# Two-layer encoder trunk: the norm's reciprocal on 128 columns by way of DRAM, a copy moved to ScalarE, one early head fewer

## The reference

```python
def rms_norm(x, g):
    return x * lax.rsqrt(jnp.mean(x * x, axis=-1, keepdims=True) + 1e-6) * g

def swiglu(h, w_gate, w_up, w_down):
    return (jax.nn.silu(h @ w_gate) * (h @ w_up)) @ w_down

# layer 0: multi-head latent attention (8 heads, rope, block-causal mask)
# layer 1: bcx = h @ w_in; y = (B * causal_conv3(C * X)) @ w_out
for i in range(2):
    h = h + mixer_i(rms_norm(h, mixer_norm_i))
    h = h + swiglu(rms_norm(h, ffn_norm[i]), w_gate[i], w_up[i], w_down[i])
return rms_norm(h, final_norm)
```

## Time and profile before

| | |
|---|---|
| median of 3 runs | 1054.24 us (1054.06 to 1055.86) |
| the profiled execution, its own time | 1052.55 us |
| its span, first to last instruction | 1050.6 us |
| TensorE busy | 1041.8 us (99%), 7018 matmuls |
| VectorE busy | 908.9 us (87%) |
| ScalarE busy | 556.6 us (53%) |
| granted TensorE clock, mean | 0.999 |
| DMA | 106.29 MB, 101 GB/s |

### The profile page before, as it was taken

How to read it: one execution, slowest core, us unless ns; L and a number is a source line. 1 busy time by engine, 2 the same in 40 slices (tenths; PEclk the granted TensorE clock), 3 DMA queues, 4 the chain that set the end, 5 groups by cost and what they waited for, 6 DMA issues and landing times. The chain is left out here.

```text
span 1050.6 us, 18481 instructions
## 1 busy us (share of the span) xinstructions
PE 1041.8 (99%) x7018; PEld 959.4 (91%) x7018; DVE 908.9 (87%) x1291; ACT 556.6 (53%) x801; POOL 46.6 (4%) x28
## 2 busy tenths in 40 slices
PE   9999999999999999999999999999999999999998
PEld 7888888899999999889888999888999999988897
DVE  6787775999999998997879988699999999899685
ACT  6678883745554555633344434355555545563432
POOL 0342230000000000000000000000000000000000
PEclk9999999999999999999999999999999999999999
DMA  8121212233233233223222332322332232223212
GB/s 339 53 71 50 75 46 80 81 121 110 92 117 120 87 113 110 75 107 121 85 107 90 111 122 80 112 90 81 120 120 93 106 120 102 88 101 120 81 71 80
DMA packets 16972, 106.29 MB, mean 101 GB/s; under 512 B 1888, under 2 KB 2272, under 8 KB 6432
## 3 DMA queue, kind: packets, MB, share of 16 engines
q1 hardware_dynamic: 16416, 104.60, 27.7%
q10 hardware_dynamic: 432, 0.83, 0.2%
q0 software_dynamic: 80, 0.26, 0.1%
HBM read 103.59 MB, written 2.10 MB: 101 GB/s over the span
## 5 line engine op out<-in xcount | busy, mean ns | idle before, releaser
L511 PE MATMUL bank<-x_hi,split 128*128 128x256 f32 (+1 forms) x704 | 203.6, 289 | 0.1
L513 PE MATMUL bank<-x_hi,split 128*128 128x256 f32 (+1 forms) x704 | 203.4, 289 | 0.0
L512 PE MATMUL bank<-x_lo,split 128*128 128x256 f32 (+1 forms) x704 | 203.3, 289 | 0.0
L511 PEld LDWEIGHTS bank<-x_hi,split 128*128 128x128 f32 x704 | 132.3, 188 | 3.4 <-DVE split L1521 0.6
L511 PE MATMUL bank<-x_hi,s_hi 128*128 128x256 f32 x480 | 134.3, 280 | 0.4 <-ACT work L1238 0.4
L513 PEld LDWEIGHTS bank<-x_hi,split 128*128 128x128 f32 x704 | 132.3, 188 | 2.5
L512 PEld LDWEIGHTS bank<-x_lo,split 128*128 128x128 f32 x704 | 132.3, 188 | 2.5
L513 PE MATMUL bank<-x_hi,s_lo 128*128 128x256 f32 x480 | 133.9, 279 | 0.0
L512 PE MATMUL bank<-x_lo,s_hi 128*128 128x256 f32 x480 | 133.8, 279 | 0.0
L1903 DVE TENSOR_TENSOR split<-raw,split 128x2048 fp32r<-128x2048 f32 x54 | 123.6, 2289 | 11.7 <-ACT split L1228 10.6
L1228 ACT ACTIVATE split<-raw 128x2048 fp32r<-128x2048 f32 x54 | 103.4, 1916 | 46.2 <-PE bank L513 25.9
(11 more groups left out here) (289 smaller groups left out, 2469.9 us busy)
## 6 DMA issues: line engine op xcount, KB each, us to landing
raw<-weights_in SPq DMA_DIRECT2D x82, 1024.0 KB, 4.8
raw<-weights_in SPq DMA_DIRECT2D x12, 768.0 KB, 4.2
work<-x SPq DMA_DIRECT2D x4, 512.0 KB, 12.9
raw<-weights_in SPq DMA_DIRECT2D x4, 512.0 KB, 3.7
out<-head SPq DMA_DIRECT2D x3, 512.0 KB, 2.7
head<-head_in SPq DMA_DIRECT2D x1, 768.0 KB, 9.3
first_raw<-weights_in SPq DMA_DIRECT2D x3, 192.0 KB, 5.4
first_raw<-weights_in SPq DMA_DIRECT2D x1, 576.0 KB, 8.0
```

The lines of the kernel that those rows point to most:

```text
L511: pe.matmul(o, lhs[0], rhs[0], start=start, stop=False, skip_group_check=True)
L512: pe.matmul(o, lhs[0], rhs[1], start=False, stop=False, skip_group_check=True)
L513: return pe.matmul(o, lhs[1], rhs[0], start=False, stop=stop, skip_group_check=True)
```

## The change

- `rms` on ScalarE takes the square root of only a quarter of the equal rows for each quarter of the tokens: rows 0 to 31 of tokens 0 to 127, rows 32 to 63 of tokens 128 to 255, and so on, in four instructions of 32x128, into `rms_part` (128x128 in SBUF). The fourth also frees the bank. The convolution uses the same function.
- `inverse_rms` on VectorE takes the reciprocal of `rms_part`, 128x128.
- SP stores `rms_part` to `rms_rows` in DRAM (64 KB), waits for it, and loads one row of each quarter back on all 128 partitions into `rstd` (256 KB in pieces of 512 B). This is `spread_inverse`, on the queue that also loads the weights, behind the fourth weight chunk of the stage. VectorE waits for it in `inverse_spread`.
- VectorE does `forms_split(0)` between the reciprocal and the wait, in all three places.
- In the channel mixer's first round, ScalarE runs a Silu of 128x1 early, and its first `gate` is written out: copy of product 1, `blocks_hi(1)`, copy of product 5, sums, copy of product 6.
- At the start of the convolution ScalarE makes the two copies of banks 0 and 1 into `mix_b`, between the copies of products 5 and 6.
- TensorE multiplies three early heads, not four, between `heads` and the wait for banks 3 and 7; the fourth comes behind `chunk_done[0]`.

```diff
+            def spread_inverse():
+                n = T.add("inverse")
+                sp.wait_ge(rms_inverted, n)
+                sp.dma_start(rms_rows, rms_part[:, :]).then_inc(inverse_stored, 16)
+                sp.wait_ge(inverse_stored, 16 * n)
+                rows = rms_rows.rearrange("(q r) n -> q r n", q=TOK)[:, 0, :]
+                sp.dma_start(rstd[:, :].rearrange("p (q n) -> p q n", q=TOK), rows.partition_broadcast(P)).then_inc(rstd_landed, 16)
...
-                c = loads(c, KF // 2, [SLOT] * 2)
+                c = loads(c, 2, [SLOT] * 2)
+                spread_inverse()
+                c = loads(c, KF // 2 - 2, [SLOT] * 2)
...
-                    c = loads(c, 8, [SLOT] * 2)
+                    c = loads(c, 2, [SLOT] * 2)
+                    spread_inverse()
+                    c = loads(c, 6, [SLOT] * 2)
...
-            output(1, 1, early[:half + 1])
+            output(1, 1, early[:half])
...
-            output(1, 1, early[half + 1:])
+            output(1, 1, early[half:])
...
-                act.activation(bank[b][:, :], bank[b][:, :], ACT.Sqrt, bias=eps[:, 0:1], scale=1.0 / width).then_inc(rms_done, 1)
+                for q in range(TOK):
+                    rows, cols = slice(q * P // TOK, (q + 1) * P // TOK), slice(q * P, (q + 1) * P)
+                    part = act.activation(rms_part[rows, :], bank[b][rows, cols], ACT.Sqrt, bias=eps[rows, 0:1], scale=1.0 / width)
+                part.then_inc(drained[b], 1)
...
+                act.activation(silu_scratch[:, :], eps[:, :], ACT.Silu)
...
-                gate(copy_first=True)
+                copy(0, 1)
+                blocks_hi(1)
+                copy(0, 5)
+                sums_hi_of(1)
+                copy(0, 6)
+                copy_last(0, 0)
...
-            act.activation(rstd[:, :], bank[6][:, :], ACT.Sqrt, bias=eps[:, 0:1], scale=1.0 / D).then_inc(drained[6], 1)
+            rms(6, D)
...
             copy(0, 5)
+            act.wait_ge(chunk_done[1], T.now("slot1") - 1)
+            for b in range(2):
+                act.activation(mix_b[b], bank[b][:, :], ACT.Copy).then_inc(drained[b], 1)
             copy(0, 6)
...
             def inverse_rms(b):
-                v.wait_ge(rms_done, T.add("rms"))
-                drain(b, v.reciprocal(rstd[:, :], bank[b][:, :]))
-                landed(b)
+                v.wait_ge(drained[b], T.add(f"b{b}"))
+                v.reciprocal(rms_part[:, :], rms_part[:, :]).then_inc(rms_inverted, 1)
+
+            def inverse_spread():
+                v.wait_ge(rstd_landed, 16 * T.add("inverse"))
...
                 inverse_rms(4)
+                forms_split(0)
+                inverse_spread()
                 scaled(3, 0)
                 scaled(4, 1)
-                forms_split(0)
                 forms(1)
...
+            inverse_rms(6)
             forms_split(0)
-            v.wait_ge(drained[6], T.add("b6"))
-            do(v.reciprocal(rstd[:, :], rstd[:, :]))
-            settle()
+            inverse_spread()
             do(v.tensor_tensor(rstd2, rstd[:, :], rstd[:, :], ALU.mult))
             settle()
             drained_part(mix_y, 2, rstd2)
-            done(1)
             for b in range(2):
-                drain(b, v.tensor_copy(mix_b[b], bank[b][:, :]))
-            landed(0, 1)
+                T.add(f"b{b}")
             split(1)
             next_forms(0)
+            landed(0, 1)
```

More of the change, by code:

```diff
@@ L222, in build @@
         rstd = sb("rstd", SEQ)
+        rms_part = sb("rms_part", P)
+        rms_rows = nc.dram_tensor("rms_rows", (P, P), F32).ap()
         acc = sb("acc", SEQ)
@@ L231, in build @@
         eps, act_scratch = numbers[:, 9 * TOK:9 * TOK + 1], numbers[:, 9 * TOK + 1:9 * TOK + 2]
+        silu_scratch = numbers[:, 9 * TOK + 2:9 * TOK + 3]
         bank = [ctx.enter_context(nc.psum_tensor(f"bank{b}", [P, SEQ], F32)) for b in range(8)]
@@ L325, in build @@
         rms_done = sem("rms_done")
+        rms_inverted, inverse_stored, rstd_landed = sem("rms_inverted"), sem("inverse_stored"), sem("rstd_landed")
         silu_done = sem("silu_done")
@@ L1400, in _ @@
             T.add("x", K_PAIRS)
-            act.wait_ge(stat_summed, T.add("stat"))
-            act.activation(rstd[:, :], bank[6][:, :], ACT.Sqrt, bias=eps[:, 0:1], scale=1.0 / D).then_inc(drained[6], 1)
+            rms(6, D)
             banks_used(dict(b6=1))
```

## The result

The changed kernel takes **1064.62 us** (median of 5 runs, 1064.13 to 1066.57), the kernel before 1054.10 (5 runs). The ratio is 1.0106, with a 95% interval of 1.0094 to 1.0117: slower by 10.5 us, where 2.4 us faster was forecast. The profiled execution took 1064.62 us with a span of 1062.8, which is 12.1 and 12.2 us above the profiled one of before. The executions of one kernel fall into groups about 1.6 us apart (the kernel before: near 1052.5, 1054.1 and 1055.8 us), so where less than 2 us is at stake the spans of profiled executions out of the lowest group are given beside the medians.

A forecast was written before the change was run, and what follows sets the result against it. TensorE, busy 99%, was taken as the bound, so only its gaps counted: heads -0.3, channel mixers -0.45 and -0.9, convolution -0.7, say -2.4 us, from 1054.24 to 1051.8 us. Range 1050.8 to 1054.4 us.

The forecast's parts named there:

- What bounds, and where the gaps are: TensorE bounds; its reachable gaps cost 0.6 (heads), 0.45 and 0.9 (channel mixers, layers 0 and 1) and 0.7 us (convolution).
- Heads (-0.3): Heads' projection: the old gap of 0.6 us goes, a new wait costs 0.3, net -0.3 us.
- copies and convolution (-0.7): Convolution: ScalarE's two copies and the smaller reciprocal make VectorE earlier, so TensorE's gap near 593 us goes, -0.7 us.
- the 3.7 us: Convolution: VectorE's time saved, 3.34 and 1.29 us less 0.9 that comes back; half was allowed to be lost.
- Reciprocal: VectorE, channel mixers: with a quarter of the columns it takes 0.9 us, where it took 3.35.
- cover of 5.1 us: Channel mixers: VectorE's work from the reciprocal's end to the end of `forms_split` hides 5.1 us of the round trip.
- ScalarE's high part: Channel mixers: `forms_split` waits for it until 216.94 us, losing 1.1 of the 2.45 us saved on VectorE.
- SP's queue: The transfers stand between the stage's fourth and fifth weight chunks; the weight load isn't late, so they cost nothing.
- Store: Round trip: storing 64 KB takes 1.7 us, upper bound 2.75.
- The load: Round trip: loading 256 KB takes 3.15 us, bounds 2.6 and 6.8; with 0.4 and the store the trip is 5.3.
- The upper bound of 6.8: Round trip: the longest load time allowed, 6.8 us, from the only load that sends one row to all partitions.
- Rival 2: Channel mixers: beyond a trip of 6.4 us each further us comes back in both; at 10 us, 1061 us; chance 8%.

## Why the prediction was wrong

- **What bounds, and where the gaps are**: right. The gaps at 178 and 593 us went with one edit each, and the kernel with a quick trip lost those at 246 and 750 us as well.
- **Heads (-0.3), copies and convolution (-0.7)**: right in the traces; each is below what the time alone can tell. In the convolution the 1.3 us of the copies were enough, so the 3.7 us that were summed up there counted for no more.
- **Reciprocal, cover of 5.1 us, ScalarE's high part**: right, each within 0.1 us. The four square roots took 1.48 us, and only the convolution felt it (0.3 us).
- **SP's queue**: "the weight load isn't late". It was issued in time (219.5 us), but behind the slow row load it landed at 229.7, where before it was 226.7. No engine waited for it, so the term stays nothing.
- **Store**: "2.7 - 1.0 = 1.7", measured 1.5. The row decided rightly against the 2.15 that the prediction worked out by the Trainium skill, page "DMA: Bandwidth & Descriptors", section "Anatomy of one DMA". That formula is a fit on DMAs that GpSimd issues, and this store goes out from SP, so the 1.5 us do not contradict the page.
- **The load**: "3.7 - 0.55 = 3.15, by the nearest rows in queue and size". This is the step that failed. The load took 8.9 to 9.8 us in the change, so the round trip was 10.4 to 11.4 us and not 5.3. The term is right within 0.3 us where the four rows lie side by side, 1, 2 or 16.5 KB apart (3.3 to 3.4 us), and wrong at 4 KB (7.0), 8 KB (9.2) and the change's 16 KB (9.1 in the median). Why DRAM answers so stays open. The term treated the load as bytes and looked at queue and size; none of the rows that it was taken from reads one small piece of DRAM for all partitions with 8 or 16 KB between its rows. The upper bound of 6.8 came from the only row that did read a shared row, and even that is too low.
- **The range** left this case out by giving it 8%. Rival 2 had the mechanism and its place, and at its trip of 10 us it said 1061; the trip was 11.4 us in layer 0, 10.7 in the convolution and 10.4 in layer 1. Its price of one microsecond per microsecond in each channel mixer is about what layer 0 shows (4.6 us for 5.0 beyond 6.4); layer 1 shows 3.1 us of gaps for 4.0. It lacked the clock, which stretched layer 1 further, and it took 0.3 us for the convolution, whose gaps grew from 0.7 to 2.7 us.
- The Trainium skill's page "DMA: Bandwidth & Descriptors", section "Latency and other measured facts", has a row on large distances: copies whose rows lie 512 KiB apart run at 207 GB/s, at 2 MiB at 164, at 4 and 8 MiB at 103, and 4 KiB of padding to the 4 MiB brings back 214. I had read it as one on large distances only. These runs agree in kind, at distances of 4 to 16 KB; here 512 B more between the rows that are read (16 B of padding to each row) are enough.

## What to carry to other kernels

A term for an operation that the trace does not show needs its access pattern matched, not only its queue and its bytes; where no row does, the chance of the bad end is not small. Rows that all partitions read belong side by side in DRAM, or 16.5 KB apart rather than 16, for example; of the distances tried, exactly 4, 8 and 16 KB were the slow ones. And a change that fails may still be right in every other part: this one is faster than the kernel before by 0.35% with one row of 2 KB (1049.61 us, span 1047.9 against 1050.6) and by 0.48% with 16 B of padding to a row (1049.78 us).

## What the runs showed of the hardware that I had not expected

- A 256 KB load of four shared 512 B rows takes 3.3 us or 9.2 by the distance of the rows: 1, 2 and 16.5 KB quick, 8 and 16 KB slow, 4 KB 7.0 us.
- What stands behind such a load on the queue is held up with it: the next 1 MB of weights took 10.2 us to land in layer 0, where it took 4.7 in the kernel before, and 8.0 with rows 4 KB apart.
- A gap of 3.0 us on TensorE in layer 1 was followed by a lower granted clock (0.61 and 0.71, above); one as long in layer 0 of the same execution was not, and in the run with four rows 16 KB apart the clock fell in layer 0 as well. The windows view around the gap of layer 0, first of the change, then of that run:

```profile
225.00:235.00 10.00, 5.49 (x45) 5.10 (x44) 6.81 (x9) 5.22 (x7) 0.00 (x0) 1.00 0.24 99
```

```profile
226.00:236.00 10.00, 6.89 (x46) 6.40 (x45) 8.50 (x10) 5.36 (x7) 0.00 (x0) 0.83 0.14 58
```

- The fall of the clock costs less than the slow stretch itself, as part of it fills time in which TensorE would have waited for its next copy. In layer 0 the run with the lower clock had a second gap of 0.8 us in place of 1.9, and VectorE's second `forms_split` behind the load (L1934) started 15.25 us behind the products in both. In layer 1 the run with rows 8 KB apart had gaps of 3.4 and 1.9 us and kept its clock at 1.00. VectorE's rows there, from the products behind the load to a later subtraction, first of the change, then of that run:

```profile
737.78 1.29 DVE L1593 TENSOR_TENSOR work<-bank,rstd 128x512 f32<-128x512 f32 x2 [5.37 <-DMA rstd<-rms_rows]
...
792.61 2.28 DVE L1934 TENSOR_TENSOR split<-raw,split 128x2048 fp32r<-128x2048 f32 x1
```

```profile
739.83 1.29 DVE L1593 TENSOR_TENSOR work<-bank,rstd 128x512 f32<-128x512 f32 x2 [5.74 <-DMA rstd<-rms_rows]
...
793.38 2.29 DVE L1934 TENSOR_TENSOR split<-raw,split 128x2048 fp32r<-128x2048 f32 x1
```

  That is 54.8 against 53.6 us: the lower clock cost layer 1 of the change about 1.3 us.
- A store of 64 KB to DRAM lands in 1.5 us, and a load of 256 KB from quick rows in 3.3. The round trip through DRAM and back to all partitions took 5.4 us in layer 0 with one row of 2 KB.
